# Norm borders with the next unit's split ahead of features and scaling; the even attention's splits, copies and windows placed apart

## The reference, cut to what matters

```python
for layer in range(2):
    if layer == 0:    # "even": differential attention and native sparse attention
        h = x @ w_in_even                      # 2840 columns
        o_a = diff_attention(...)              # 4 heads, two softmaxes each
        o_b = nsa_attention(...)               # compressed, selected and window keys, three gates
        mix = concatenate([o_a, o_b]) @ w_out_even
    else:             # "odd": forgetting attention, 16 heads
        h = x @ w_in_odd                       # 3088 columns
        mix = forgetting_attention(...) @ w_out_odd
    x = layer_norm(ALPHA * x + mix, gain[layer, 0], bias[layer, 0])
    x = layer_norm(ALPHA * x + square(relu(x @ w_up)) @ w_down, gain[layer, 1], bias[layer, 1])

def compress(t, j):   # inside nsa_attention: blocks of 32 tokens, every 16, through a small MLP
    blocks = t[:, cmp_idx] + pe[j]
    return gelu(blocks @ w1[j] + b1[j]) @ w2[j]
```

## Time and profile before

| | us |
|---|---|
| median of 3 runs | 2418.59 (2415.63 to 2419.69) |
| profiled execution | 2421.92 |
| its span | 2420.3 |
| PE busy | 2267.6 (94%) |
| DVE busy | 1044.1 (43%) |
| ACT busy | 702.8 (29%) |
| POOL busy | 95.3 (4%) |
| mean granted clock of PE | 0.963 of 2.4 GHz |

### The profile page before, as it was taken

How to read it: one execution, slowest core, us unless ns; L and a number is a source line. 1 busy time by engine, 2 the same in 40 slices (tenths; PEclk the granted TensorE clock), 3 DMA queues, 4 the chain that set the end, 5 groups by cost and what they waited for, 6 DMA issues and landing times.

```text
span 2420.3 us, 28281 instructions
## 1 busy us (share of the span) xinstructions
PE 2267.6 (94%) x11771; PEld 1665.7 (69%) x11771; DVE 1044.1 (43%) x1906; ACT 702.8 (29%) x1189; POOL 95.3 (4%) x96
## 2 busy tenths in 40 slices
PE   8999899979989899899878999999999999999998
PEld 7866687864433333488556688888878777888887
DVE  5347465342322323433666464234351465432335
ACT  4324354320000000222336323124133363331330
POOL 2001001000000000000000010000000000000001
PEclk9989999989999999999869999999999999999999
DMA  5232242268999999722010223232232201323220
GB/s 197 87 127 85 79 158 103 84 233 365 426 427 428 426 427 427 281 92 80 25 46 1 82 94 102 90 105 87 70 135 87 87 2 35 122 88 105 92 99 35
DMA packets 106739, 370.32 MB, mean 153 GB/s; under 512 B 15040, under 2 KB 20672, under 8 KB 94320
## 3 DMA queue, kind: packets, MB, share of 16 engines
q1 hardware_dynamic: 103584, 361.65, 39.7%
q0 software_dynamic: 3024, 6.83, 0.9%
HBM read 368.38 MB, written 4.19 MB: 154 GB/s over the span
## 4 chain that ended last, share of the span: by engine, by line
PE 80%; DMA 9%; DVE 7%; ACT 2%; issue 1%; POOL 0%; SPq 0%; DVEq 0%; ACTq 0%; POOLq 0%
PE PB L455 53%; PE PB L1902 9%; PE PB L472 5%; PE PB L774 4%; PE PB L465 3%; PE PB L666 3%; DMA Z<-in_w_exp_gate 3%; DMA FH_raw<-in_w_exp_gate 3%; DMA FL_raw<-in_w_exp_gate 1%; DMA Z<-in_w_exp_down 1%; PE PB L790 1%; PE PB L671 1%; DVE W L447 1%; DVE X L2193 1%; ACT nsp L700 1%
## 5 line engine op out<-in xcount | busy, mean ns | idle before, releaser
L455 PE MATMUL PB<-W,FH 128*128 128x512 f32 (+1 forms) x1792 | 556.3, 392 | 11.5 <-DVE FL L828 6.7
L447 DVE TENSOR_TENSOR W<-R,W 128x2048 fp32r<-128x2048 f32 (+1 forms) x128 | 291.3, 2277 | 623.7 <-ACT W L439 623.6
L439 ACT ACTIVATE W<-R 128x2048 fp32r<-128x2048 f32 (+1 forms) x128 | 243.4, 1902 | 634.2 <-PE PB L455 629.9
L455 PEld LDWEIGHTS PB<-W,FH 128*128 128x128 f32 x1792 | 330.9, 189 | 79.8 <-DVE FL L828 8.1
L455 PE MATMUL PB<-W,hid 128*128 128x512 f32 x1536 | 349.4, 390 | 0.0
L455 PE MATMUL PB<-W,FL 128*128 128x512 f32 (+1 forms) x896 | 348.2, 389 | 0.0
L455 PE MATMUL PB<-FH,W 128*128 128x512 f32 (+1 forms) x1152 | 327.9, 370 | 6.3 <-DVE W L447 6.3
L455 PEld LDWEIGHTS PB<-W,hid 128*128 128x128 f32 x1536 | 288.2, 188 | 59.7
L455 PEld LDWEIGHTS PB<-FH,W 128*128 128x128 f32 x1152 | 211.7, 192 | 41.9 <-issue 7.1
L455 PE MATMUL PB<-FL,W 128*128 128x512 f32 (+1 forms) x576 | 212.6, 369 | 0.0
L455 PEld LDWEIGHTS PB<-W,FL 128*128 128x128 f32 x896 | 169.2, 189 | 34.9
(11 more groups left out here) (334 smaller groups left out, 2612.1 us busy)
## 6 DMA issues: line engine op xcount, KB each, us to landing
R<-in_mlp_w_up SPq DMA_DIRECT2D x32, 1024.0 KB, 5.3
R<-in_mlp_w_down SPq DMA_DIRECT2D x32, 1024.0 KB, 5.1
Z<-in_w_exp_down SPq DMA_DIRECT2D x14, 2048.0 KB, 29.2
Z<-in_w_exp_up SPq DMA_DIRECT2D x13, 2048.0 KB, 35.2
R<-in_w_exp_gate SPq DMA_DIRECT2D x11, 2048.0 KB, 32.3
W_raw<-in_w_exp_up SPq DMA_DIRECT2D x10, 2048.0 KB, 31.5
R<-in_w_exp_up SPq DMA_DIRECT2D x9, 2048.0 KB, 30.7
R<-in_w_in SPq DMA_DIRECT2D x12, 1024.0 KB, 5.8
```

The lines of the kernel that those rows point to most:

```text
L439: k.A.e.activation(w.splits[w.split_of[u]][0][:, 0:m], w.rows(u), ACT.Copy).then_inc(*w.hi.tick(u))
L447: k.V.e.tensor_tensor(wl[:, 0:m], w.rows(u), wh[:, 0:m].bitcast(F32), ALU.subtract).then_inc(*w.lo.tick(u))
L455: ins = te.matmul(bank, l, r, start=(start and n == 0), stop=(stop and n == len(terms) - 1), skip_group_check=True)
```

## The change

Five things. (1) In the two out-projection borders (`act_out_ln`, `dve_out_ln`) and the MLP's (`act_mlp`, `dve_mlp`), ACT's and DVE's split of the next unit stand ahead of the features of tile 1 (ACT) and ahead of these and of the third tile's scaling (DVE); the split behind it follows the third tile's scaling instead of the fourth tile's centring. (2) In `dve_out_ln` the adds and first statistics of all tiles precede the second split, in the order 1, 0, 2, 3. (3) PE's transposes of the fourth tile move one group of matmuls later in the MLP (after group 2 instead of 1) and one step later in the odd projection. (4) In the last even panel the two copies to partitions 64 to 127 go to ACT, with a new wait of DVE on them before it doubles the keys; the bank of the transposes is free only after the doubling. (5) In the attention's list the windows block is two slots of four instructions, one before and one behind the first pair of block 2, and the two cuts move from the blocks of two key chunks (i = 1) to those of four (i = 3).

```diff
--- before.py
+++ after.py
@@ -1238,8 +1238,8 @@
     act_cut(k, u0 + 2)
     act_cut(k, u0 + 3)
     act_features(k, ("ln", n), 0)
+    act_cut(k, u0 + 4)
     act_features(k, ("ln", n), 1)
-    act_cut(k, u0 + 4)
     act_cut(k, u0 + 5)
     act_features(k, ("ln", n), 2)
     act_features(k, ("ln", n), 3)
@@ -1314,20 +1314,20 @@
 def dve_out_ln(k, name, n):
     u0 = k.start[name]
     dve_cut(k, u0 + 2)
-    dve_cut(k, u0 + 3)
-    for i in range(NT):
+    for i in (1, 0, 2, 3):
         dve_add(k, name, 0, i, ALPHA)
         dve_ln_half(k, n, i)
+    dve_cut(k, u0 + 3)
     for i in range(NT):
         dve_add(k, name, 1, i, ALPHA)
         dve_ln_center(k, n, i)
+        if i == 2:
+            dve_cut(k, u0 + 4)
         if i in (1, 2):
             dve_features(k, ("ln", n), i - 1)
-        if i == 3:
-            dve_cut(k, u0 + 5)
         dve_ln_scale(k, n, i)
         if i == 2:
-            dve_cut(k, u0 + 4)
+            dve_cut(k, u0 + 5)
     dve_features(k, ("ln", n), 2)
     dve_features(k, ("ln", n), 3)
 
@@ -2286,11 +2286,12 @@
         nsa[i, g] = pairs(seq)
     k.last3 = ("even", m - 1)
     d3, d2, d1, d0 = [diff[i] for i in (3, 2, 1, 0)]
-    return ([("ks", 3)] + d3[0:2] + [("five", 0), ("five", 1), d3[2], ("five", 2), ("five", 3), d3[3], ("windows",), d2[0],
-             ("hidden", 0), d2[1], ("hidden", 1), d2[2], ("hidden", 2), d2[3], ("hidden", 3), ("dn", 3), d1[0], d1[1],
+    return ([("ks", 3)] + d3[0:2] + [("five", 0), ("five", 1), d3[2], ("five", 2), ("five", 3), d3[3], ("windows", 0), d2[0],
+             ("windows", 1), ("hidden", 0), d2[1], ("hidden", 1), d2[2], ("hidden", 2), d2[3], ("hidden", 3), ("dn", 3), d1[0], d1[1],
              ("biased",), d1[2], ("small",), d1[3], ("kc",), d0[0], d0[1], ("dn", 2), d0[2], d0[3], ("few", 3)]
-            + nsa[3, 0] + [("dn", 1), ("few", 2)] + nsa[3, 1] + [("dn", 0)] + nsa[2, 0] + [("few", 1)] + nsa[2, 1]
-            + nsa[1, 0] + [("few", 0), ("cut", 0)] + nsa[1, 1] + [("cut", 1)] + nsa[0, 0] + nsa[0, 1]
+            + nsa[3, 0][0:2] + [("cut", 0)] + nsa[3, 0][2:] + [("dn", 1), ("few", 2)] + nsa[3, 1][0:2] + [("cut", 1)]
+            + nsa[3, 1][2:] + [("dn", 0)] + nsa[2, 0] + [("few", 1)] + nsa[2, 1] + nsa[1, 0] + [("few", 0)] + nsa[1, 1]
+            + nsa[0, 0] + nsa[0, 1]
             + [("out", 0), ("out", 1), ("out", 2)])
 
 
@@ -2312,7 +2313,7 @@
         pe_turn(k, ("even", p, i), k.nsp[i], k.rope_rows.at(p, i))
 
     def fours(i):
-        pe_doubled(k, "four", i, k.dve_step.at("four", i), Banks.FLIPS)
+        pe_doubled(k, "four", i, k.kk_doubled.at("ks", i), Banks.FLIPS)
         if i:
             pe_doubled(k, "ks", i - 1, k.kk_out.at("ks", i - 1), Banks.FLIPS)
 
@@ -2334,7 +2335,7 @@
     T, u0 = k.T, k.start["compress"]
     if q == 0:
         k.banks.take(T, ("hidden",), k.dve_step.at("biased"), hold=True)
-        T.wait_ge(*k.dve_step.at("windows"))
+        T.wait_ge(*k.dve_step.at("windows", 1))
     units = [u0 + 2 * j + q // 2 for j in range(2)]
     for u in units:
         T.wait_ge(*k.w.landed[u % RAW].at(u))
@@ -2474,6 +2475,7 @@
                 A.wait_ge(*k.rope_rows.at(3, 3))
                 ae.activation(rows, bank[:], ACT.Copy).then_inc(*k.four_copied.tick(i))
             elif p == 5:
+                act_fours(k, i)
                 if i:
                     act_doubled(k, "ks", i - 1)
                 A.wait_ge(*k.kk_doubled.at("ks", i))
@@ -2483,6 +2485,16 @@
                 act_piece(k, ("even", last[p], i), dst[last[p]], i)
         if p < 5:
             act_cut(k, u0 + 2 * p + 3)
+
+
+def act_fours(k, i):
+
+    k.A.wait_ge(*k.kk_turned.at("four", i))
+    b4 = k.banks["four", i][:].rearrange("p (j g t) -> p j g t", j=2, g=2)
+    lo = 128 * i - 1 if i else 0
+    for j in range(2):
+        ins = k.A.e.activation(k.cs[64:128, j, :, lo:128 * i + 127], b4[64:128, j, :, (0 if i else 1):128], ACT.Copy)
+    ins.then_inc(*k.act_step.tick("four", i))
 
 
 def act_doubled(k, which, i):
@@ -2597,14 +2609,13 @@
     V, ve, rows = k.V, k.V.e, even_rows(k, i)
     V.wait_ge(*k.kk_turned.at("four", i))
     b4 = k.banks["four", i][:].rearrange("p (j g t) -> p j g t", j=2, g=2)
-    lo = 128 * i - 1 if i else 0
     for j in range(2):
-        ve.tensor_copy(k.cs[0:64, j, :, 128 * i:128 * i + 128], b4[0:64, j])
-        ins = ve.tensor_copy(k.cs[64:128, j, :, lo:128 * i + 127], b4[64:128, j, :, (0 if i else 1):128])
+        ins = ve.tensor_copy(k.cs[0:64, j, :, 128 * i:128 * i + 128], b4[0:64, j])
     ins.then_inc(*k.dve_step.tick("four", i))
     V.wait_ge(*k.kk_doubled.at("four", i))
     V.settle(rotate(k, rows[:, 256:384].rearrange("p (h d) -> p h d", h=2), k.rope[:, i, 0:8], k.rope[:, i, 8:16],
                     rows[:, 0:64], 2))
+    V.wait_ge(*k.act_step.at("four", i))
     twice(k, k.double["ks"][i], rows[:, 256:384]).then_inc(*k.kk_doubled.tick("ks", i))
 
 
@@ -2618,18 +2629,18 @@
     twice(k, k.double["kw"][i], rows[:, 0:128]).then_inc(*k.kk_doubled.tick("kw", i))
 
 
-def dve_windows(k):
+def dve_windows(k, j):
 
     k.V.wait_ge(*k.projected.at("even", 5, 3))
     k.V.wait_ge(*k.dve_step.at("four", 3))
-    for j in range(2):
-        for g in range(2):
-            for h in range(2):
-                src = k.cs[:, j, g, 16 * h:16 * h + 512].rearrange("p (n c) -> p c n", c=16)[:, 0:16:2, :]
-                dst = k.windows[j][:, 512 * h:512 * h + 512].rearrange("p (l c) -> p l c", l=8)[:, :, 32 * g:32 * g + 32]
-                ins = k.V.e.tensor_tensor(dst, src, k.pe[:, j, 8 * h:8 * h + 8].unsqueeze(2).to_broadcast([P, 8, 32]),
-                                          ALU.add)
-    ins.then_inc(*k.dve_step.tick("windows"))
+    k.V.wait_ge(*k.act_step.at("four", 3))
+    for g in range(2):
+        for h in range(2):
+            src = k.cs[:, j, g, 16 * h:16 * h + 512].rearrange("p (n c) -> p c n", c=16)[:, 0:16:2, :]
+            dst = k.windows[j][:, 512 * h:512 * h + 512].rearrange("p (l c) -> p l c", l=8)[:, :, 32 * g:32 * g + 32]
+            ins = k.V.e.tensor_tensor(dst, src, k.pe[:, j, 8 * h:8 * h + 8].unsqueeze(2).to_broadcast([P, 8, 32]),
+                                      ALU.add)
+    ins.then_inc(*k.dve_step.tick("windows", j))
 
 
 def dve_hidden_turned(k):
@@ -2729,7 +2740,7 @@
             elif kind == "five" and what == "score":
                 dve_fives(k, i)
             elif kind == "windows" and what == "score":
-                dve_windows(k)
+                dve_windows(k, i)
             elif kind == "biased" and what == "score":
                 V.wait_ge(*k.pe_step.at("windows", 3))
                 ve.tensor_tensor(k.hrow, k.banks["hidden",][:, 0:256], k.b1, ALU.add).then_inc(*k.dve_step.tick("biased"))
@@ -2838,7 +2849,7 @@
                     ins = products(te, banks[f][:, at], terms, half == 0 and at.start == 0, half == 1)
                     if half == 1 and at.stop == S:
                         ins.then_inc(*k.projected.tick("up", layer, c, j, f))
-                    if first and at.stop < S and (half, f) in ((0, 3), (1, 1)):
+                    if first and at.stop < S and (half, f) in ((0, 3), (1, 2)):
                         pe_ln(k, 2 * layer, 2 + half)
                 if half == 0 and at.stop == S:
                     ins.then_inc(*w.half_used.tick(u))
@@ -2890,9 +2901,8 @@
                     act_hid(k, layer, c, j, f - 1)
             act_hid(k, layer, c, j, 3)
         for n in range(8):
-            if layer == 0 and c and n == 6:
-                act_features(k, ("ln", 1), 0)
-                act_features(k, ("ln", 1), 1)
+            if layer == 0 and c and n >= 6:
+                act_features(k, ("ln", 1), n - 6)
             if u0 + 10 + n < end:
                 act_cut(k, u0 + 10 + n)
         if layer == 0 and c:
@@ -2937,13 +2947,13 @@
                     V.wait_ge(*k.added.at(layer, c, half, i))
                     (dve_ln_center if half else dve_ln_half)(k, n_ln, i)
                 if (c, half) == (1, 1):
+                    if layer == 0 and i == 2:
+                        dve_cut(k, u0 + 16)
                     if layer == 0 and i in (1, 2):
                         dve_features(k, ("ln", 1), i - 1)
-                    if layer == 0 and i == 3:
-                        dve_cut(k, u0 + 17)
                     dve_ln_scale(k, n_ln, i)
                     if layer == 0 and i == 2:
-                        dve_cut(k, u0 + 16)
+                        dve_cut(k, u0 + 17)
             if (c, half) != (1, 1):
                 dve_cut(k, u0 + 13 + 4 * half)
             elif layer == 0:
@@ -3008,7 +3018,7 @@
         pe_project(k, "odd", p, u0 + 2 * p, NT, lambda i: featured(k, ("ln", 1), i),
                    lambda i: (k.panel_a if p < 4 else k.panel_v).at("odd", p, i), after=(turn(p - 1) if 1 <= p < 5 else None),
                    steps=(None if p else FEATURED_LATE),
-                   behind={0: {1: lambda: pe_ln(k, 1, 2), 2: lambda: pe_ln(k, 1, 3)}, 1: {1: turn_gates}}.get(p, {}))
```

(1 more changed line is left out.)

## The result

| | before | after |
|---|---|---|
| median of 4 runs on one chip, us | 2417.64 | 2390.73 |
| ratio, 95% interval | | 0.989 (0.9873 to 0.9907) |
| profiled execution, us | 2421.92 | 2388.91 |
| its span, us | 2420.3 | 2387.6 |
| PE busy, us | 2267.6 | 2245.6 |

The account below looks back on a forecast made before the run. PE, busy 94% of the span, was taken to bound the kernel through stops and lower clock. Terms 1.3 + 4.6 + 10.6 - 4.4 + 4.5 + 2.2 + 3.4 = 22.2 us took the median 2418.59 to 2396.4; range 2387 to 2408.

Parts of the forecast that it names:

- What bounds it: Whole kernel: PE busy 94% of the span; edits pay where PE stands or runs at its lower clock, possible after stops.
- Copies: Last even panel: two of four key-row copies on ACT let PE's transposes start at 1157.5 instead of 1158.88, 1.3 us.
- Windows: Attention: the windows block in halves brings the transposes of block 2's second pair to 1189.5 from 1194.12, 4.6 us.
- Old places: Attention, where the two splits stood: less idle time and less work at the lower clock, 6.8 and 3.8, together 10.6 us.
- New places: Attention, block of four key chunks: DVE has hardly any room, so the two splits lose 1.9 and 2.5, together -4.4 us.
- Even border: Even norm border: MLP starts 2.27 us earlier, clock does not fall (2.6), later last transposes cost 0.35; 4.5 us.
- Middle border: Middle norm border: DVE's split starts at 1765.5 instead of 1767.65, PE at 1767.75 instead of 1769.99; 2.2 us.
- Odd border: Odd norm border: as the even one with a shorter stretch at the lower clock, 2.27 + 1.5 - 0.35 = 3.4 us.
- Rival (a): Whole kernel: stops shrink but every stretch at clock 0.50 remains, the sum loses 9.9, 2406.3 us; chance 0.15.
- (b): Attention: the splits only change place, their cost equals what they leave, 6.2 less gain, 2402.6 us; chance 0.10.
- (c): Block of four chunks: a split stops PE, the clock falls and stays low, 22 us longer, 2424.6 us; chance 0.04.
- (d): All edits: the next DVE wait replaces each; only the borders' idle gain, 3 x 2.2, remains, 2412 us; chance 0.04.

Follow-up runs that it names:

- e2: The kernel before with the two splits of the attention moved and nothing else; ratio 0.9945 (0.9926 to 0.9964), 13.3 us faster.
- e10: The changed kernel itself once more, with no further change; ratio 0.9887 (0.987 to 0.9903), 2390.16 us.

## Why the prediction was right, and where it was off

The direction and the mechanism hold, and the time lies in the range (2387 to 2408). The forecast time was 5.7 us too high, 1.0 of it because the median before is 2417.64 with the fourth run, with errors of both signs in the rest. The range's lower end doesn't follow from what it names: both bounds of windows and copies and new places at 2.0 give 2396.4 - 0.7 - 1.1 - 2.4 = 2392.2, and 2390.7 lies below that, so the 5 us of room under it were luck. Two of the prediction's own signs of being wrong came: a clock row at a border still shows 0.50, and the attention is 18.3 us shorter, not 10.

- **What bounds it.** Right: PE's stops and the clock behind them. It was said that after a stop PE "may" run slow; how often, the prediction didn't weigh.
- **Copies, 1.3.** 1.7 to the key transposes, and 1.2 more right behind them: a stop of 2.43 was followed by a fall 5 times in 5, one of 1.67 only 3 times in 9. The term left the clock out. The table load ran 1.28 us, and the next activation started 1.30 after its start, with no drain here either, where the Trainium skill (ScalarE: Activation LUTs, What ACT_TABLE_LOAD costs) has one of about 1380 ns.
- **Windows, 4.6.** Stops as traced (1.45, 2.65), and in the one trace of after 4.2 us, but over all profiles 2.3. The apply behind the first stop did run at the upper clock. What failed is that the new stop of 2.65 was taken to be followed by full clock, when the clock fell there in 6 of 8 profiles and the second pair came 1.5 us later, and that the start was compared with the one trace of before, the longest of its group (22.38 us, others down to 20.97).
- **Old places, 10.6.** 16.4, by e2 in that part alone. Idle time 9.1 against 6.5, clock 7.3 against 4.1. I had priced the two stops and the few rows right behind each. The stretch at half clock behind the second stop was longer than the 2.4 us priced, about 3.4. Left out were the stops behind both and a third stretch at half clock, from 1349 to 1355.9, behind a stop of 1.12 us. In the second and the third of these stretches the spreads took 1.92 us, not 1.04. Rows of before, behind those of the earlier trace rows:

```profile
1343.26 1.92 PE L790 MATMUL PB<-ident,stat 128*64 128x128 f32 x16
1347.33 0.49 PE L666 MATMUL PB<-Z 64*128 64x128 f32 x4 [1.12 <-DVE Z L815]
...
1353.87 1.92 PE L790 MATMUL PB<-ident,stat 128*64 128x128 f32 x16
```

  In after the whole stretch stands at 1.00. The sum over the stretch, busy and idle, would have shown this before the prediction.
- **New places, -4.4.** Right in the trace of after (-3.7: stops of 1.85, 2.11, 1.63 and 1.35 where 1.9 each was said); in six other profiles the first one costs 1.6 more through the clock (-5.4). The 0.43 us ahead of this stretch come on top.
- **Even border, 4.5.** To the MLP 2.02 (2.27 said): ACT's half waits until PE frees its buffer, DVE then 0.57 for ACT, which makes the stop 2.12 and not 1.7. The failed step is "1.7 us, below the 2.69 that the middle border passes at 1.00, so I take no fall": one row of one execution was made a threshold. 2.68 was followed by a fall in 3 of 6 profiles. So 1.1 of the 2.6 for the clock came in this trace. The last transposes cost 0.41 (0.35 said). Together 2.7.
- **Middle border, 2.2.** 1.86; DVE waits for ACT here as well.
- **Odd border, 3.4.** 2.18 to the MLP and 1.05 behind it, 3.2; the clock stayed up in this trace, as was said, by luck.

Rival (a), that the clock doesn't come back, is half true at the borders and wrong in the attention. (b), that the splits only change place, is refuted by e2: 16.4 for 5.8. (c) never came: in the block of four chunks the clock fell for some 3 us, in e10 for 7, and came back. (d) is refuted by the one-part kernels. The sum with measured terms, 2.9 + 2.3 + 16.4 - 5.5 + 2.7 + 1.9 + 3.2 = 23.9, stands against 26.9 by the medians, whose interval is 22.5 to 30.7. It is near the forecast's 22.2 because the 5.8 us that the old places gave beyond their price were mostly offset by the windows, the new places and the borders.

## What to carry to other kernels

A stop of PE costs itself and, in more than half of the cases from 2 us on, mostly 1.2 to 2.6 us behind it; price the whole stretch, idle and busy, from mark to mark, and not stop by stop. Put work for a side engine not where the list has room for a slot but where that engine's own rows show idle time longer than the work and PE is late for another reason. And before reading a term off two traces, look at how far unchanged stretches differ between them.

## What was not expected of the hardware

- In code that no edit touched, one and the same stretch took 99.12 to 102.38 us in four profiles. PE's busy time in it ran from 78.5 to 82.9 us with where the clock fell, and its idle time from 19.3 to 21.2 (the 0.43 of e2 left out).
- In the attention, where the earlier trace rows has its second row, the clock stood at 0.50 for some 27 to 37 us in all, in every one of the 14 profiles, with PE busy up to 5.00 of 5 us. No experiment here touches it.
- A fall behind a stop of 2.1 us at an MLP cost the same 1.49 us in all 7 cases (7.32 against 5.83 for 48 matmuls); behind 3.15 it cost 1.3 to 2.6.
- Matmuls without use in the stop kept the clock up in all of 6 cases, and the MLP started no later by more than 0.1 us.
- The stretch ahead of all edits ended 8 us apart in different profiles.
